# A branch for the first layer's head: order of the first products, the centring of tile 2

## The chip, the cores and the metric

The kernel runs on one core of a Trainium2 chip. The metric is the device time of one execution in microseconds, median over runs. Five engines work at once, each on its own list of instructions, and wait for each other through semaphores: TensorE (PE, with its weight loads as PEld), VectorE (DVE), ScalarE (ACT), GpSimd (POOL) and SyncE (SP), which here only issues transfers.

## The reference

A two-layer encoder on 512 tokens of 1024 channels. What bears on the change is its start: a layer norm of the input, and the input projection of the first layer.

```python
h = layer_norm(x, ln_in_g, ln_in_b)
for l in range(DEPTH):
    proj = h @ w_in[l]
    a_q, a_k, a_v, b_u, b_b, b_c, c_u, d_q, d_k, d_v = split_columns(proj)
    ...                       # four groups of heads, each RMS-normalised, side by side in mix
    h = layer_norm(DN_ALPHA * h + mix @ w_out[l], ln1_g[l], ln1_b[l])
    ffn = jnp.square(jax.nn.relu(h @ w1[l])) @ w2[l]
    h = layer_norm(DN_ALPHA * h + ffn, ln2_g[l], ln2_b[l])
```

## The kernel before

**Tiles.** The tokens lie in four tiles of 128 rows, the channels in eight blocks of 128 (kt 0 to 7). The stream x is held with tokens on the partitions; for a product it is turned by TensorE (eight transposes for a tile, four for each half of 512 channels), into PSUM banks 4 and 5, and copied from there as two operands: ScalarE casts the high part h_hi (line 860), VectorE subtracts it from the bank for the low part h_lo (line 1254). Weights come in blocks of 128 x 2048, and are split the same way: ScalarE casts w_hi (line 838, in parts of 512 columns at the start), GpSimd subtracts for w_lo (line 1708). A product of full precision is three of these: high by high, low by high, high by low weights. Block 0 of the weights serves kt 0 to 3, block 1 kt 4 to 7.

**The input norm.** Per tile VectorE takes two statistics (1201), their aggregate (1208) and the variance with its epsilon (1210); GpSimd raises it to the power -1/2 (rstd, 1687); VectorE centres and multiplies by the gain in two halves (1279) and scales and adds the bias in two halves (1284). Gain and bias stand on one partition each; TensorE spreads them to 128 rows at the start by 16 transposes (499) into banks 2 and 3 (gain) and 6 and 7 (bias). Bank 2 is where tile 2's product goes later, bank 3 tile 3's, so ScalarE copies the gain to SBUF (rows, 903), and tiles 2 and 3 centre with that copy, tiles 0 and 1 with the banks. The order by hand on VectorE: norm 0, statistics 1, low parts of tile 0, norm 1, statistics 2, low parts of tile 1, and so on; the low parts of tile 3 stand inside the layer loop, behind a wait for the parameters (cols, qk_gain) that GpSimd's queue loads.

**TensorE's order.** Behind the spreading stand 8 filler transposes (keep_warm, 493), the turn of tile 0, 6 more, and then the loop over the two layers (505). In it, tile 0 and tile 1 take their products with high weights first: for each kt the high part (521) and the low part (522), the turn of tile 1 ahead of kt 4 of tile 0. Then come the eight products with low weights of tile 0 (530), the turn of tile 2, the eight of tile 1, and tiles 2 and 3 with all three at once (449 to 451), tile 3's turn in the middle of tile 2. Both layers run this code. Tile 0 of the second layer is turned in the last chunk of the first layer's MLP, under an If on the layer (790). The MLP's middle chunks are a loop of their own (826).

**The names in the order listings.** A row is an instruction or a run of equal ones, as the compiled program has them; MATMUL stands for a weight load and its product. REGISTER_ALU and ISA are register steps that a semaphore's target takes, COMPARE_AND_BRANCH is what an If or a loop's end becomes.

## Time and profile before

| | us |
|---|---|
| median of 3 runs | 1070.64 |
| lowest and highest | 1070.27, 1070.86 |
| the profiled execution | 1070.55 |
| its span | 1068.9 |

| engine | busy, share of the span |
|---|---|
| PE | 99% |
| PEld | 84% |
| DVE | 73% |
| ACT | 49% |
| POOL | 9% |

The span runs from the first to the last instruction; 1.65 us of the profiled execution lie around it. The profile is of one execution. Its timeline gives each instruction, or run of like ones, with its start from the span's beginning and its duration; products overlap their weight loads, so for TensorE the starts of loads tell the order better than the busy time, in which a product counts 0.39 us though the next starts 0.23 later. A remark in brackets is the idle time of that engine ahead of the row and what ended it; "issue" means that nothing in the profile was waited for.

### The profile page before, as it was taken

To read this page: it belongs to the slowest core of one execution; us is meant where nothing else is said; L and a number is where in the kernel's file an instruction comes from. 1 tells how busy PE (TensorE), PEld (TensorE's weight loads), DVE (VectorE), ACT (ScalarE), POOL (GpSimd) and SP (SyncE) were. 2 spreads that over 40 slices of the span, in tenths; PEclk is the share of its full clock that TensorE was granted. 3 is DMA by queue.
4 is the path that set the end of the run, shared out by engine and by line. 5 is a ranking of instruction groups with operands and counts; after the bars stand their busy time and mean duration, and the time that the engine had idled before them with its cause. 6 is when DMAs were issued, how large, how long until landed. Compare 5 with 4: busy or idle time off the path is not lost.

```text
span 1068.9 us, 15589 instructions
## 1 busy us (share of the span) xinstructions
PE 1054.0 (99%) x5310; PEld 896.7 (84%) x5310; DVE 785.4 (73%) x1090; ACT 521.9 (49%) x784; POOL 92.6 (9%) x84
## 2 busy tenths in 40 slices
PE   8999999999999999999999999999999999999996
PEld 6888889998888888888888888899888888888885
DVE  8855886968757758758887568777794784784787
ACT  3433666365355355355634247653643643642652
POOL 5200232100000000000002003221000000000001
PEclk9999999999999999999999999999999999999998
DMA  7432013030521520431343410310234134024122
GB/s 288 158 118 78 2 61 120 2 126 32 205 79 40 179 97 31 169 115 42 117 147 134 158 40 21 118 41 23 105 120 156 40 118 158 39 98 178 40 78 80
DMA packets 17385, 105.54 MB, mean 99 GB/s; under 512 B 2019, under 2 KB 2707, under 8 KB 5795
## 3 DMA queue, kind: packets, MB, share of 16 engines
q1 hardware_dynamic: 15984, 98.70, 25.3%
q0 software_dynamic: 1184, 5.86, 1.7%
q8 instruction: 40, 0.66, 0.2%
q14 instruction: 33, 0.25, 0.1%
q10 hardware_dynamic: 144, 0.07, 0.0%
HBM read 101.49 MB, written 2.10 MB: 97 GB/s over the span
## 4 chain that ended last, share of the span: by engine, by line
PE 98%; DVE 0%; issue 0%; DVEq 0%
PE bank L449 19%; PE bank L451 18%; PE bank L450 18%; PE bank L756 10%; PE bank L758 9%; PE bank L757 9%; PE bank L699 4%; PE bank L685 2%; PE bank L458 1%; PE bank L596 1%; PE bank L597 1%; PE bank L530 1%; PE bank L609 1%; PE bank L521 1%; PE bank L522 1%; PE bank L675 0%
## 5 line engine op out<-in xcount | busy, mean ns | idle before, releaser
L449 PE MATMUL bank<-h_hi,w_hi 128*128 128x512 f32 (+1 forms) x704 | 260.6, 370 | 0.0
L450 PE MATMUL bank<-h_lo,w_hi 128*128 128x512 f32 (+1 forms) x704 | 260.3, 370 | 0.0
L451 PE MATMUL bank<-h_hi,w_lo 128*128 128x512 f32 (+1 forms) x704 | 260.3, 370 | 0.0
L756 PE MATMUL bank<-w_hi,hid_hi 128*128 128x512 f32 x448 | 174.4, 389 | 0.0
L757 PE MATMUL bank<-w_lo,hid_hi 128*128 128x512 f32 x448 | 174.3, 389 | 0.0
L758 PE MATMUL bank<-w_hi,hid_lo 128*128 128x512 f32 x448 | 174.3, 389 | 0.0
L1167 DVE TENSOR_TENSOR w_lo<-w_raw,w_hi 128x2048 fp32r<-128x2048 f32 x62 | 141.9, 2288 | 36.8 <-ACT w_hi L873 30.0
L451 PEld LDWEIGHTS bank<-h_hi,w_lo 128*128 128x128 f32 x704 | 132.6, 188 | 22.6
L450 PEld LDWEIGHTS bank<-h_lo,w_hi 128*128 128x128 f32 x704 | 132.7, 188 | 22.4
L449 PEld LDWEIGHTS bank<-h_hi,w_hi 128*128 128x128 f32 x704 | 132.6, 188 | 22.3
L873 ACT CAST w_hi<-w_raw 128x2048 fp32r<-128x2048 f32 x56 | 107.1, 1913 | 78.8 <-PE bank L758 56.4
L1581 DVE TENSOR_TENSOR x<-bank,x 128x512 f32<-128x512 f32 x112 | 74.9, 686 | 45.1 <-PE bank L758 45.1
L758 PEld LDWEIGHTS bank<-w_hi,hid_lo 128*128 128x128 f32 x448 | 84.1, 188 | 17.6
L757 PEld LDWEIGHTS bank<-w_lo,hid_hi 128*128 128x128 f32 x448 | 84.1, 188 | 17.4
L756 PEld LDWEIGHTS bank<-w_hi,hid_hi 128*128 128x128 f32 x448 | 84.1, 188 | 17.3
L1076 ACT ACTIVATE y<-bank 128x512 f32<-128x512 f32 x64 | 38.2, 597 | 105.7 <-PE bank L451 105.7
L1555 DVE TENSOR_TENSOR hid_sum<-y 128x256 f32<-128x256 f32 x64 | 24.3, 421 | 43.3 <-ACT y L1078 43.2
L1186 DVE TENSOR_TENSOR w_raw<-w_third,w_raw 128x2048 f32<-128x2048 f32 x24 | 54.8, 2285 | 1.6 <-DMA w_third<-in_weights 1.6
L1570 DVE TENSOR_TENSOR hid_lo<-hid_sum,hid_hi 128x1024 fp32r<-128x1024 f32 x32 | 39.2, 1226 | 22.4 <-ACT hid_hi L1089 22.4
L1479 DVE SCALAR_TENSOR_TENSOR x<-bank,group_r,x 128x512 f32<-128x512 f32 x64 | 46.8, 747 | 10.3 <-PE bank L451 9.5
L1684 POOL DMA_DIRECT2D rows<-in_rows x4 | 2.3, 570 | 579.7 <-DVE hid_lo L1570 579.4
L449 PE MATMUL bank<-w_hi,mix_hi 128*128 128x512 f32 x128 | 50.9, 398 | 0.0
(174 smaller groups left out, 1643.1 us busy)
## 6 DMA issues: line engine op xcount, KB each, us to landing
w_raw<-in_weights SPq DMA_DIRECT2D x63, 1024.0 KB, 4.8
w_third<-in_weights SPq DMA_DIRECT2D x23, 1024.0 KB, 4.8
rows<-in_rows POOLq DMA_DIRECT2D x4, 1024.0 KB, 5.1
w_raw<-in_weights SPq DMA_DIRECT2D x4, 512.0 KB, 7.7
out_h<-x SPq DMA_DIRECT2D x8, 256.0 KB, 2.0
x<-in_x SPq DMA_DIRECT2D x3, 512.0 KB, 9.7
dft<-in_dft SPq DMA_DIRECT2D x2, 512.0 KB, 7.1
qk_gain<-in_qk_gain POOLq DMA_DIRECT2D x3, 192.0 KB, 3.3
```

What stands on the lines that cost most here:

```text
L449: pe.matmul(dst, s_hi, m_hi, start=first, stop=False)
L450: pe.matmul(dst, s_hi, m_lo, start=False, stop=False)
L451: return pe.matmul(dst, s_lo, m_hi, start=False, stop=last)
L699: last = pe.matmul(bank[4 + (u // 4) % 2][:, c:c + HEAD_DIM], pT[:, u % 2, i * P:(i + 1) * P], v, start=(i == 0), stop=(i == k1 - k0 - 1))
L756: pe.matmul(bank[dst + t][:], s_hi, m_hi, start=start, stop=False, skip_group_check=goes_on)
L757: pe.matmul(bank[dst + t][:], s_hi, m_lo, start=False, stop=False, skip_group_check=goes_on)
L758: done = pe.matmul(bank[dst + t][:], s_lo, m_hi, start=False, stop=stop, skip_group_check=goes_on)
L873: act.copy(w_hi[:, SLOT[i], :], raw_of(i)).then_inc(sems["w_hi"], 1)
L1167: dve.tensor_tensor(w_lo[:, SLOT[i % CHUNK_OPERANDS], :], raw_of(i), w_hi[:, SLOT[i % CHUNK_OPERANDS], :].bitcast(F32), ALU.subtract).then ...
L1186: dve.tensor_tensor(dst, a, b, ALU.subtract).then_inc(sems["w_sum"], 1)
L1479: dve.scalar_tensor_tensor(out=xs, in0=b[:], scalar=group_r[:, g, t:t + 1], in1=xs, op0=ALU.mult, op1=ALU.add)\
L1581: dve.tensor_tensor(xs, bank[dst + t][:], xs, ALU.add).then_inc(sems["added"], 1)
```

## The change

It touches TensorE's order and VectorE's, and adds no computation.

- Of the 8 filler transposes ahead of tile 0's turn one is left; the 6 behind it go.
- The first products of a layer stand in two branches on the layer. The second, for l > 0, keeps the order of before, but asks for h_hi ahead of a high part and for h_lo ahead of a low part, where before h_lo was asked for ahead of both. The first, for l < 1, has an order of its own: high, low and low-weight products for kt 0 and 1, high and low for kt 2 to 7, and only then tile 1's turn; two low-weight products, all high then all low parts of tile 1, low-weight products, tile 2's turn ahead of the last six.
- VectorE takes the first low half of tile 0 between the two statistics of tile 1, and the second behind tile 1's variance.
- Tile 2 centres with the gain in banks 2 and 3, like tiles 0 and 1; tile 3 alone uses the copy.

```diff
--- before.py
+++ after.py
@@ -499,36 +499,67 @@
                         last = pe.transpose(first_row(which, half)[:, c * P:(c + 1) * P],
                                             first[:, k:k + 1].to_broadcast([P, P]), ident)
                     last.then_inc(first_spread, 1)
-            keep_warm(8)
+            keep_warm(1)
             turn(0, 0)
-            keep_warm(6)
             with pe.Fori(0, DEPTH) as l:
 
                 def first_group(t, kt):
                     c = slice(t * P, (t + 1) * P)
                     return (bank[t][:], h_hi[:, kt, c], h_lo[:, kt, c], *w_cols(kt // 4, kt % 4, BANK, 0, BANK))
 
-
-                for t in range(2):
-                    for kt in range(KT):
-                        if t == 0 and kt == 4:
-                            turn(l, 1)
+                def own_high(t, kts):
+                    for kt in kts:
+                        if kt % 4 == 0:
+                            wait(pe, l, "h_hi", 2 * t + kt // 4 + 1)
+                        if t == 0:
+                            high_part_ready(l, kt // PARTS, kt % PARTS)
+                        dst, t_hi, _, m_hi, _ = first_group(t, kt)
+                        pe.matmul(dst, t_hi, m_hi, start=kt == 0, stop=False)
+
+                def own_low(t, kts):
+                    for kt in kts:
                         if kt % 4 == 0:
                             wait(pe, l, "h_lo", 2 * t + kt // 4 + 1)
-                        if t == 0:
-                            high_part_ready(l, kt // PARTS, kt % PARTS)
-                        dst, t_hi, t_lo, m_hi, _ = first_group(t, kt)
-                        pe.matmul(dst, t_hi, m_hi, start=kt == 0, stop=False)
+                        dst, _, t_lo, m_hi, _ = first_group(t, kt)
                         pe.matmul(dst, t_lo, m_hi, start=False, stop=False)
-                for t in range(2):
-                    for kt in range(KT):
+
+                def weights_low(t, kts):
+                    for kt in kts:
                         if t == 0:
                             part_ready(l, kt // PARTS, kt % PARTS)
-                        if t == 1 and kt == 0:
-                            turn(l, 2)
                         dst, t_hi, _, _, m_lo = first_group(t, kt)
-                        last = pe.matmul(dst, t_hi, m_lo, start=False, stop=kt == KT - 1)
-                    last.then_inc(sems["products"], 1)
+                        done = pe.matmul(dst, t_hi, m_lo, start=False, stop=kt == KT - 1)
+                        if kt == KT - 1:
+                            done.then_inc(sems["products"], 1)
+
+                with pe.If(l < 1):
+
+                    own_high(0, range(2))
+                    own_low(0, range(2))
+                    weights_low(0, range(2))
+                    for kt in range(2, KT):
+                        own_high(0, (kt,))
+                        own_low(0, (kt,))
+                    turn(l, 1)
+                    weights_low(0, range(2, 4))
+                    own_high(1, range(KT))
+                    own_low(1, range(KT))
+                    weights_low(0, range(4, 6))
+                    weights_low(1, range(4))
+                    turn(l, 2)
+                    weights_low(0, range(6, KT))
+                    weights_low(1, range(4, KT))
+                with pe.If(l > 0):
+
+                    for t in range(2):
+                        for kt in range(KT):
+                            if t == 0 and kt == 4:
+                                turn(l, 1)
+                            own_high(t, (kt,))
+                            own_low(t, (kt,))
+                    weights_low(0, range(KT))
+                    turn(l, 2)
+                    weights_low(1, range(KT))
                 for t in range(2, TOK):
                     for kt in range(KT):
                         if kt == KT // 2 and t + 1 < TOK:
@@ -1267,7 +1298,7 @@
             def first_norm(t):
 
                 def row(which, half):
-                    if which or t < 2:
+                    if which or t < TOK - 1:
                         dve.wait_ge(first_spread, 2 * which + half + 1)
                         return first_row(which, half)[:]
                     dve.wait_ge(first_kept, half + 1)
@@ -1289,8 +1320,12 @@
                 row_stats(0, n)
             variance(0, 2, 1, LN_EPS)
             first_norm(0)
-            input_stats(1)
-            stream_low(0, 0, 0)
+            dve.wait_ge(x_landed[1], 16)
+            row_stats(1, 0)
+            low_half(0, 0, 0, 0)
+            row_stats(1, 1)
+            variance(1, 4, 2, LN_EPS)
+            low_half(0, 0, 0, 1)
             first_norm(1)
             input_stats(2)
             stream_low(0, 0, 1)
```

TensorE, from the end of the spreading to its first products of layer 0, before:

```order
L493 MATMUL bank<-ident_first 128x128 x8
L458 MATMUL bank<-ident_first,x 128x128 [waits normed]
L458 MATMUL bank<-ident_first,x 128x128 x3
L458 MATMUL bank<-ident_first,x 128x128 [waits normed]
L458 MATMUL bank<-ident_first,x 128x128 x3
L493 MATMUL bank<-ident_first 128x128 x6
L505 UNCONDITIONAL_BRANCH
L505 ISA
L323 ISA [waits h_lo]
L521 MATMUL bank<-w_hi,h_hi 128x512 [waits w_hi_part]
L522 MATMUL bank<-w_hi,h_lo 128x512
```

And now:

```order
L493 MATMUL bank<-ident_first 128x128
L458 MATMUL bank<-ident_first,x 128x128 [waits normed]
L458 MATMUL bank<-ident_first,x 128x128 x3
L458 MATMUL bank<-ident_first,x 128x128 [waits normed]
L458 MATMUL bank<-ident_first,x 128x128 x3
L504 UNCONDITIONAL_BRANCH
L535 COMPARE_AND_BRANCH
L323 ISA
L323 ISA [waits h_hi]
L517 MATMUL bank<-w_hi,h_hi 128x512 [waits w_hi_part]
L323 REGISTER_ALU
L517 MATMUL bank<-w_hi,h_hi 128x512 [waits w_hi_part]
```

The fillers are gone but one, a compare stands ahead of the products, and the first one waits for h_hi and a part of w_hi, with h_lo asked for behind two high parts.

VectorE from tile 0's last scaling to tile 1's centring, before:

```order
L1284 SCALAR_TENSOR_TENSOR x<-x,rstd,bank 128x512 [waits first_spread,centred]
L1201 BN_STATS bn<-x 128x6 [waits x_landed1]
L1201 BN_STATS bn<-x 128x6
L1208 BN_AGGR moments<-bn 128x2 [waits stats,x_landed1]
L1210 TENSOR_SCALAR var_eps<-moments 128x1 [waits moments]
L1254 TENSOR_TENSOR h_lo<-bank,h_hi 128x4x128 [waits h_hi] x2
L1279 SCALAR_TENSOR_TENSOR x<-x,moments,bank 128x512 [waits first_spread,moments]
```

And now:

```order
L1315 SCALAR_TENSOR_TENSOR x<-x,rstd,bank 128x512 [waits first_spread,centred]
L1232 BN_STATS bn<-x 128x6 [waits x_landed1]
L1285 TENSOR_TENSOR h_lo<-bank,h_hi 128x4x128 [waits h_hi]
L1232 BN_STATS bn<-x 128x6
L1239 BN_AGGR moments<-bn 128x2 [waits stats,x_landed1]
L1241 TENSOR_SCALAR var_eps<-moments 128x1 [waits moments]
L1285 TENSOR_TENSOR h_lo<-bank,h_hi 128x4x128 [waits h_hi]
L1310 SCALAR_TENSOR_TENSOR x<-x,moments,bank 128x512 [waits first_spread,moments]
```

The first low half has moved between the statistics, so the variance, for which GpSimd's rstd waits, has one more operation ahead of it.

TensorE at the end of layer 0's branch and the start of the other, now (before there was no such place):

```order
L531 MATMUL bank<-w_lo,h_hi 128x512 [waits w_lo_part]
L531 MATMUL bank<-w_lo,h_hi 128x512 [waits w_lo]
L531 MATMUL bank<-w_lo,h_hi 128x512 x4
L535 UNCONDITIONAL_BRANCH
L552 COMPARE_AND_BRANCH
L323 ISA
L323 ISA [waits h_hi]
L517 MATMUL bank<-w_hi,h_hi 128x512 [waits w_hi_part]
L524 MATMUL bank<-w_hi,h_lo 128x512 [waits h_lo]
```

In layer 1 the compare of line 535 jumps here, over the 128 loads and products of the first branch and some 15 register steps and waits; in layer 0 the compare of line 552 jumps over the second branch, which is as long.

## Rows read from the trace of the kernel before

**Rows 1.** Waits of TensorE, whole span: us in total, times, longest.

```profile
PE bank L521 <- DVE h_lo L1254: 0.4, 1, 0.4
PE bank L458 <- DVE x L1284: 0.4, 1, 0.4
```

**Rows 2.** Timeline, weight loads (PEld): start, us, line, operation, count, idle before.

```profile
7.64 1.72 PEld L493 LDWEIGHTS bank<-ident_first 128*128 128x128 f32 x8
9.35 1.28 PEld L458 LDWEIGHTS bank<-ident_first,x 128*128 128x128 f32 x8
...
11.91 0.19 PEld L521 LDWEIGHTS bank<-w_hi,h_hi 128*128 128x128 f32 x1 [0.63 <-issue]
...
14.40 0.42 PEld L458 LDWEIGHTS bank<-ident_first,x 128*128 128x128 f32 x4 [0.80 <-DVE x L1284]
15.06 0.42 PEld L458 LDWEIGHTS bank<-ident_first,x 128*128 128x128 f32 x4 [0.24 <-DVE x L1284]
...
17.36 0.19 PEld L521 LDWEIGHTS bank<-w_hi,h_hi 128*128 128x128 f32 x1 [0.23 <-DVE h_lo L1254]
...
22.70 1.02 PEld L458 LDWEIGHTS bank<-ident_first,x 128*128 128x128 f32 x8
...
25.40 0.19 PEld L449 LDWEIGHTS bank<-w_hi,h_hi 128*128 128x128 f32 x1
```

**Rows 3.** Timeline, VectorE (DVE), first 32 us.

```profile
7.34 1.57 DVE L1284 SCALAR_TENSOR_TENSOR x<-x,rstd,bank 128x512 f32<-128x512 f32 x2
8.83 1.28 DVE L1201 BATCH_NORM_STATS2 bn<-x 128x6 f32<-128x512 f32 x2
...
12.29 1.40 DVE L1279 SCALAR_TENSOR_TENSOR x<-x,moments,bank 128x512 f32<-128x512 f32 x2
13.61 1.40 DVE L1284 SCALAR_TENSOR_TENSOR x<-x,rstd,bank 128x512 f32<-128x512 f32 x2
...
17.82 3.37 DVE L1279 SCALAR_TENSOR_TENSOR x<-x,moments,rows 128x512 f32<-128x512 f32 x2
...
26.70 1.40 DVE L1284 SCALAR_TENSOR_TENSOR x<-x,rstd,bank 128x512 f32<-128x512 f32 x2
```

**Rows 4.** ScalarE's timeline; weight transfers: issues of line 361, time to landing.

```profile
10.47 1.07 ACT L860 CAST h_hi<-bank 128x512 fp32r<-128x512 f32 x2 [1.85 <-PE bank L458]
11.43 3.23 ACT L838 CAST w_hi<-w_raw 128x512 fp32r<-128x512 f32 x6
...
L361 SPq DMA_DIRECT2D w_raw<-in_weights x4: 424/436/440, 1.8 to 3.7; - x4
...
DMA to landing us min/median/max: 4.8/5.7/8.9
```

**Rows 5.** GpSimd's timeline (POOL); then the landing of qk_gain, last parameter.

```profile
12.14 5.04 POOL L1708 TENSOR_TENSOR w_lo<-w_raw,w_hi 128x512 fp32r<-128x512 f32 x4 [0.90 <-ACT w_hi L838]
...
17.64 3.00 POOL L1708 TENSOR_TENSOR w_lo<-w_raw,w_hi 128x512 fp32r<-128x512 f32 x2
...
21.30 0.54 POOL L1679 DMA_DIRECT2D qk_gain<-in_qk_gain  x1
...
DMA to landing us min/median/max: 6.5/6.5/6.5
```

**Rows 6.** Line 1279 by source of its gain row: ns min/median/max.

```profile
L1279 DVE SCALAR_TENSOR_TENSOR x<-x,moments,bank x4: 737/741/749, 6.0 to 12.9; 128x512 f32<-128x512 f32 x4
L1279 DVE SCALAR_TENSOR_TENSOR x<-x,moments,rows x4: 743/1208/1780, 17.8 to 26.0; 128x512 f32<-128x512 f32 x4
```

**Rows 7.** TensorE's branches, layer loop (505), chunk loop (826): ns min/median/max.

```profile
L505 PEldq COMPARE_BRANCH  x2: 76/1772/3467, 532.5 to 1055.0; - x2
...
L826 PEldq COMPARE_BRANCH  x4: 79/159/247, 368.1 to 973.4; - x4
```

**Rows 8.** Timeline, start of layer 1: weight loads, then ScalarE (ACT).

```profile
536.26 0.19 PEld L521 LDWEIGHTS bank<-w_hi,h_hi 128*128 128x128 f32 x1 [0.37 <-issue]
...
540.99 0.19 PEld L521 LDWEIGHTS bank<-w_hi,h_hi 128*128 128x128 f32 x1 [0.33 <-DVE h_lo L1254]
...
539.62 1.07 ACT L860 CAST h_hi<-bank 128x512 fp32r<-128x512 f32 x2 [1.72 <-PE bank L458]
```


## The prediction

> **What bounds the kernel now.** I began with the waits of TensorE. The reader is to see that they are almost nothing: behind the landing of its first operand only two stand in the whole span, 0.4 us each [rows 1]. TensorE's stream is therefore the bound, and a change can pay only by what it does to gaps in that stream or to its length. The order of the stream in time was read next, from the weight loads, one per product [rows 2]. It has its gaps in the head of the first layer: the first product starts at 11.91, eight products later the engine stands until 14.40 and 15.06 for the two halves of tile 1, and again until 17.36. From there on it never stands for another engine in that layer. The mark for everything below is 25.40, the first product of tile 2: what is gained there is gained to the end, unless something later becomes late. VectorE's rows show who sets those stops [rows 3]: one unbroken chain of normalisations from 8.83 to 28.10.
>
> **Durations used.** A warm product of 512 columns takes its place every 0.227 us: eight from 22.70 back to 20.88. A turn of eight transposes among them takes 0.88 more (22.70 to 25.40 is 2.70: eight products and a turn). A restart after a stop costs 0.10 once, and in a steady run a load starts one place ahead of its product. From the end of VectorE's work to TensorE's load it is 0.05 (15.01 to 15.06). The eight fillers from 7.64 to 9.35 come every 0.214 us, twice the 0.11 of later transposes, so that is the lower level, 1.2 GHz, though the granted clock is given as 1.00 throughout; the eight transposes from 9.35 take 1.28, half at either pace, so the rise falls at about 10.1. ScalarE starts its cast of a half 1.12 after the half's turn starts, where the fourth transpose was the last slow one (9.35 to 10.47); I take 1.15 for slow ones.
>
> **Part 1, tile 0's turn.** Seven of the eight filler transposes ahead of it go, and all six behind. Tile 0's halves are normalised at 8.09 and 8.91 (7.34 and 1.57 for the pair, 0.75 for the first) [rows 3], so their turns start at 8.14 and 8.96, in place of 9.35 and some 0.8 later. ScalarE casts the first half from 9.29 to 9.88 and the second from 10.11, where it cast both from 10.47 [rows 4]. Its six weight casts, 0.52 apart, start at 10.59 in place of 11.43 and end at 13.81; the fifth needs a transfer issued at 3.7 that was at most 8.9 on its way, so there by 12.6 [rows 4], and would start at 12.67. TensorE can multiply own high parts from 10.0 (only h_hi asked for), not 11.91.
>
> **Part 2, VectorE around tile 1.** The low half moves between the two statistics. VectorE does the same sum of work: first statistics from 8.83, low half at 9.91 behind ScalarE's cast (0.4 idle, much as before), second statistics to 11.20, variance at 11.53, second low half at 11.61, centring at 12.20, in place of 12.29 [rows 3]. The variance is now 1.1 later, and that is the added wait: GpSimd's rstd of tile 1 stands ahead of its low weight parts. It starts at 11.84 and delays the four parts that began at 12.14 [rows 5] by 0.22, to 12.36. They are asked for late enough: block 0 is complete at 14.9 and needed at 15.37. The rstd is there at 12.4, VectorE asks at 13.52. Tile 1 is normalised at 14.26 and 14.92, 0.09 sooner than before.
>
> **Part 3, what fits ahead of tile 1.** Before, 8 products stood ahead of its turn; now 18 do (16 own, 2 with low weights). Followed one by one: two high at 10.0, low at 10.66 once VectorE's half is out (10.60), low weights at 11.23 and 11.46, the rest from 11.69, each waiting for nothing until kt 7, whose cast ends at 13.81. The last goes in at 14.20, its slot ends at 14.43; tile 1's first half was ready at 14.31, the second's turn waits until 14.98 anyway. All ten extra products vanish into the old stop: 10 x 0.227 = 2.27. Behind that turn stand 30 products and tile 2's turn, where 40 and a turn stood. The first load is at 15.37, so the mark falls at 15.37 + 0.10 + 29 x 0.227 + 0.88 = 22.93, in place of 25.40: 2.47 sooner. Beside the ten products that is VectorE's 0.09 and some 0.1 of the stop at 17.36, which goes: high parts come first there, and the low half is out 0.4 before it is asked for. I take 2.45.
>
> **Part 4, tile 2's centring.** This is what keeps part 3 alive. With the gain row in SBUF the two operations took 3.37, from PSUM they take 1.41: singly 0.74 against up to 1.78 [rows 3, 6]. The pair from PSUM that counts is that at 12.29, which ran in the midst of GpSimd's subtractions [rows 5] and took 1.40 all the same, so I take that and no slowing. VectorE then has tile 2 normalised at 19.8 and 20.45, in place of 22.51. TensorE asks at 20.93. With the old centring it would have stood until 22.4, and 1.5 of the gain would be gone. VectorE's low half of tile 2 comes at 22.88, TensorE needs it at 22.93: no slack, but no loss. Tile 3 is normalised at 25.45 and 26.11, in place of 28.10, and asked for at 25.66 and 26.22. Next is its low half, which waits for the parameters: they land at 27.8 (issued at 21.3, 6.5 on their way) [rows 5], so it is out at 28.4, and TensorE gets there at 29.5. That is 1.0 of cover.
>
> **Part 5, the branches.** Layer 1 keeps its order but must jump over layer 0's. At its start TensorE has run dry: the jump back takes 3.47, and the first load waits until 536.26 with 0.37 idle [rows 7, 8]. So the added jumps are bare: one taken, 0.25, and one not taken, 0.08, by the chunk loop's [rows 7], with a register step or two 0.39 in all. Most of that is met by the stop at 540.99, where TensorE waits 0.33 for tile 1's low half. That half hangs on ScalarE, which starts its cast only at 539.62 after its own jump [rows 8], well behind tile 1's turn (538.7 even when late), so it stays where it is. Net 0.2 lost; bounds 0 and 0.4. In layer 0 both jumps pass while TensorE has work queued: nothing. The Trainium skill, Advanced Engine Details and Errata, Control Flow Timing, has about 0.11 for a compare-and-branch; two of them would make the net 0.05 in place of 0.2, and the rows' larger price is what I take.
>
> **Sum.** 2.45 less 0.2 is 2.25. The profiled execution took 1070.55 for a span of 1068.9; the median of the three runs is 1070.64, 0.09 above it. 1070.64 - 2.25 = **1068.4**. Bounds: the first cast 0.1 later or sooner moves the chain by as much; a clock that rises 1 us later slows up to five products and costs up to 0.4; the jump 0 to 0.4. So 1067.9 to 1069.1 for this case.
>
> **The rivals.**
> - *The clock stays low.* The fillers held TensorE busy without a break until the rise at about 10.1. Now it stands some 0.1 to 0.3 three times from 8.06 on. The Trainium skill, TensorE: Matmul & The Clock Gate, Part 1, wants sustained activity before the higher level and says that the point varies from run to run. Which of the two the trace bears out it doesn't say, since TensorE never stood there before; the stops are short. No row tells how long the low level would last. Through nine of the 18 products, at 0.45 in place of 0.227, it costs 2.0, of which waits ahead of 11.7 hide 0.5: 1069.9, the price I take. Through all 18 it is 4.1 less 0.6: 1071.9.
> - *Layer 1's branch isn't at hand.* The loop's jump back cost 3.47 because its code had to be fetched [rows 7]; the chunk loop's, whose code was there, 0.25. If the jump over layer 0's order (128 loads and multiplies and some 15 waits) leaves the code just fetched, it costs 3.47 in place of 0.25 with nothing queued: 1068.4 + 3.2 = 1071.6, slower than before. It decides from the point at which the else branch lies beyond the fetched piece; two such fetches give 1075. Against: some 145 instructions are little beside the chunk loop's 360 products with their loads, which its jump spans for 0.25. The Trainium skill, Advanced Engine Details and Errata, ISA Cache, gives 256 instructions to a line of code; by it loop start and branch would share one, and the next line would have to be there some 40 instructions on, which is narrow.
> - *The first part doesn't fit.* ScalarE's casts or the transfer behind them slip by some tenths; each tenth passes through. 0.4 to 0.8 lost: 1069.0.
> - *The centring gains nothing.* If reading PSUM beside GpSimd cost as much as SBUF, 1.5 of the gain goes: 1069.9. The pair at 12.29 speaks against it.
>
> **How the numbers follow.** Forecast 0.62, clock 0.10, branch not at hand 0.10, first part slipping 0.15, centring 0.03. A measurement tells 0.2% from no change, 2.14 us, so faster means below 1068.5, and the forecast lies just there. Of its 0.62 some 0.46 fall below that, and 0.02 of the slipping case: faster 0.48. Slower needs above 1072.8: half of the branch case, 0.05 at most. Same 0.47. The range reaches from 1067.9 to 1070.1, which leaves out the branch case and some tails.
>
> **What would show it.** In the changed profile: first product's load near 10.0; turn of tile 1 at 14.3 and 15.0 with 18 products ahead; both centrings of tile 2 at 0.74 and GpSimd's last pair of subtractions back from 3.00 to 2.55 [rows 5]; first product of tile 2 at 22.9 to 23.0 and no idle after it in that layer; in layer 1 TensorE's idle at the loop's start grown from 0.37 to 0.7 to 0.8 and the wait for h_lo gone. Wrong it is if the pace of transposes is still 0.213 beyond 10.2, if tile 2's or 3's turn shows idle for VectorE, or if more than 1 us opens around 533 to 541.

## The result: slower by 0.3%

| | before | changed |
|---|---|---|
| median, us | 1070.3 (11 runs) | 1073.87 (11 runs) |
| lowest and highest | 1069.89, 1070.86 | 1071.17, 1076.16 |
| the profiled execution | 1070.55 | 1074.24 |
| its span | 1068.9 | 1072.6 |
| mean granted clock of TensorE in it | 0.997 | 0.993 |

The ratio is 1.0029, interval 1.0021 to 1.0037. The forecast was 1068.4 and its range ended at 1070.1; the time went the other way. The runs also lie wider apart than those of before: 5.0 us instead of 1.0.

**The waits of TensorE** in the changed kernel, whole span (us in total, times, longest). Behind the landing of the first operand, where [rows 1] have two waits of 0.4, there is one big one (3.9 counts from the end of the last product; from the last load it is 4.34):

```profile
PE bank L517 <- issue: 3.9, 1, 3.9
```

"Issue" means that nothing in the profile was waited for. Where it lies, the timeline tells. First the head of layer 0: weight loads of the changed kernel (start, us, line, count, idle before), for [rows 2]:

```profile
10.06 0.40 PEld L517 LDWEIGHTS bank<-w_hi,h_hi 128*128 128x128 f32 x2 [0.30 <-issue]
10.71 0.30 PEld L524 LDWEIGHTS bank<-w_hi,h_lo 128*128 128x128 f32 x2 [0.25 <-DVE h_lo L1285]
...
13.96 0.19 PEld L517 LDWEIGHTS bank<-w_hi,h_hi 128*128 128x128 f32 x1 [0.19 <-ACT w_hi L869]
...
14.38 1.08 PEld L458 LDWEIGHTS bank<-ident_first,x 128*128 128x128 f32 x8
15.43 0.30 PEld L531 LDWEIGHTS bank<-w_lo,h_hi 128*128 128x128 f32 x2
...
23.04 0.19 PEld L449 LDWEIGHTS bank<-w_hi,h_hi 128*128 128x128 f32 x1
```

The mark, the first product of tile 2, stands at 23.04 and not at 25.40: the head has gained 2.36. A mark of one execution also holds the moment at which TensorE's clock rose in it. Two versions of experiments 2 and 3 that run the old order in the head (both_branches and skip1) had their first transposes faster and the mark at 25.07 and 24.82. So marks compare to some 0.5, unless the transposes ran alike; in the two profiles here both ran late to full pace. VectorE and GpSimd there, for [rows 3, 5]:

```profile
9.96 0.69 DVE L1285 TENSOR_TENSOR h_lo<-bank,h_hi 128x512 fp32r<-128x512 f32 x1 [0.40 <-ACT h_hi L891]
...
17.80 1.40 DVE L1310 SCALAR_TENSOR_TENSOR x<-x,moments,bank 128x512 f32<-128x512 f32 x2
...
22.27 1.29 DVE L1285 TENSOR_TENSOR h_lo<-bank,h_hi 128x512 fp32r<-128x512 f32 x2
```

```profile
11.84 0.55 POOL L1722 TENSOR_TENSOR rstd<-var_eps,half_neg 128x1 f32<-128x1 f32 x1 [1.49 <-DVE var_eps L1241]
12.37 5.06 POOL L1743 TENSOR_TENSOR w_lo<-w_raw,w_hi 128x512 fp32r<-128x512 f32 x4
...
17.90 2.54 POOL L1743 TENSOR_TENSOR w_lo<-w_raw,w_hi 128x512 fp32r<-128x512 f32 x2
```

So the head did what was forecast of it. Now the start of layer 1, for [rows 8]. Weight loads of the changed kernel:

```profile
533.38 0.19 PEld L789 LDWEIGHTS bank<-w_hi,hid_lo 128*128 128x128 f32 x1
537.90 0.29 PEld L517 LDWEIGHTS bank<-w_hi,h_hi 128*128 128x128 f32 x1 [4.34 <-issue]
538.07 0.34 PEld L524 LDWEIGHTS bank<-w_hi,h_lo 128*128 128x128 f32 x1
538.50 0.33 PEld L517 LDWEIGHTS bank<-w_hi,h_hi 128*128 128x128 f32 x1
...
542.89 0.19 PEld L517 LDWEIGHTS bank<-w_hi,h_hi 128*128 128x128 f32 x1
...
544.60 0.19 PEld L517 LDWEIGHTS bank<-w_hi,h_hi 128*128 128x128 f32 x1
```

and the two loads of the kernel before that answer to 533.38 and 542.89:

```profile
535.71 0.19 PEld L758 LDWEIGHTS bank<-w_hi,hid_lo 128*128 128x128 f32 x1
...
538.98 0.19 PEld L521 LDWEIGHTS bank<-w_hi,h_hi 128*128 128x128 f32 x1
```

What stands still is the sequencer. The branches of TensorE, as they answer to [rows 7] (ns min/median/max, then first and last start): line 504 is the loop's jump back, 535 the branch for l < 1, 552 that for l > 0.

```profile
L504 PEldq COMPARE_BRANCH  x2: 76/1944/3812, 530.2 to 1058.7; - x2
...
L535 PEldq COMPARE_BRANCH  x2: 82/1720/3357, 9.2 to 534.2; - x2
...
L552 PEldq COMPARE_BRANCH  x2: 73/154/236, 20.6 to 537.6; - x2
```

The jump back takes 3.8, much as before (3.47). Behind it the new jump over layer 0's branch takes 3357 ns, from 534.2 on, and the first load of layer 1 follows 0.4 behind its end. The last row says that the same kind of jump, over the other branch, took 236 ns in layer 0, at 20.6. On the queue that carries code (the rows don't say for which engine), one piece is moved in the stretch 535.0 to 535.5, inside those 3357 ns (packets, MB, share):

```profile
q8 instruction: 1, 0.02, 11.8%
```

In the version of experiment 1 one piece is moved between 533.5 and 534.0, again within 1.5 of the end of the jump back, but products run meanwhile. Both profiles count 40 pieces in the whole span. By these rows the changed kernel fetches no more than that version; it stands still for a piece that the other gets while it works.

Last, the clock. The same stretches of the changed kernel and of the version of experiment 1, in which TensorE doesn't stop there (us; busy and count of PE, PEld, DVE, ACT, POOL; granted clock, DMA share, GB/s):

```profile
530.00:534.00 4.00, 3.99 (x21) 3.04 (x19) 4.00 (x8) 2.16 (x4) 0.00 (x0) 1.00 0.01 4
534.00:538.00 4.00, 0.09 (x1) 0.10 (x1) 3.27 (x7) 1.52 (x4) 0.99 (x1) 0.75 0.33 78
538.00:543.00 5.00, 5.00 (x17) 4.15 (x17) 0.00 (x0) 0.42 (x1) 0.00 (x0) 0.52 0.95 372
543.00:548.00 5.00, 5.00 (x25) 4.13 (x23) 4.80 (x8) 0.76 (x2) 0.00 (x0) 1.00 0.02 8
```

```profile
534.00:538.00 4.00, 4.00 (x24) 3.37 (x23) 3.31 (x7) 2.14 (x4) 0.99 (x1) 1.00 0.37 111
538.00:543.00 5.00, 5.00 (x24) 4.12 (x23) 5.00 (x9) 0.00 (x0) 0.00 (x0) 1.00 1.03 362
```

The clock falls to the lower of its two levels (1.2 GHz, 0.50), while TensorE stands: in stretches of 0.5 us it is 1.00 up to 535.5, 0.97 in the next and 0.50 from 536.0 on, and it is back between 542.75 and 543.0. The loads behind the stop come 0.42 to 0.43 apart, where a warm product takes 0.227.

**The account**, from the loads of both profiles:

| point | before | changed | difference |
|---|---|---|---|
| first product of tile 2, layer 0 | 25.40 | 23.04 | -2.36 |
| last load of layer 0 | 535.71 | 533.38 | -2.33 |
| first load of layer 1 | 536.26 | 537.90 | +1.64 |
| first load behind eight products and a turn | 538.98 | 542.89 | +3.91 |
| first product of tile 1, layer 1 | 540.99 | 544.60 | +3.61 |
| span | 1068.9 | 1072.6 | +3.7 |

The jump costs 3.97 (1.64 and 2.33), the low clock 2.27 (4.99 instead of 2.72 for the same eight products and turn), and the stop of before at 540.99 gives 0.30 back. All 2.36 of the head arrive at the end of layer 0, and are outweighed there within five microseconds.

### The profile page after: what moved, and what is told of

Read it like the earlier page. It is cut to its first block, busy times and chain, and to the rows that moved or that the text cites. A ratio compares the mean times of both kernels' runs of the same rounds, so it can differ in the third digit from the quotient of the medians.

```text
span 1072.6 us, 15573 instructions
## 1 busy us (share of the span) xinstructions
PE 1054.5 (98%) x5297; PEld 896.7 (84%) x5297; DVE 783.6 (73%) x1090; ACT 523.3 (49%) x784; POOL 92.2 (9%) x84
## 4 chain that ended last, share of the span: by engine, by line
PE 98%; issue 1%; DMA 0%; DVE 0%; DVEq 0%
PE bank L449 18%; PE bank L450 18%; PE bank L451 18%; PE bank L788 9%; PE bank L789 9%; PE bank L787 9%; PE bank L730 4%; PE bank L716 2%; PE bank L458 1%; PE bank L627 1%; PE bank L628 1%; PE bank L517 1%; PE bank L524 1%; PE bank L531 1%; PE bank L640 1%
```

## The experiments

The theory after the two traces: the jump's target lies in a piece of code that isn't at hand in layer 1, and the fetch is bare. The rivals: the cost is that of any branch behind the jump back; the cost hangs on the length of the jump; and, for the head, that the gain isn't the order's.

### 1. The branches exchanged (swap)

The code for l > 0 now stands first, that for l < 1 behind it. The order in each layer is that of the changed kernel.

```diff
+                with pe.If(l > 0):
+                    ...       # the old order
                 with pe.If(l < 1):
                     ...       # the new order
-                with pe.If(l > 0):
-                    ...       # the old order
```

> The changed kernel with its two branches in the other sequence in the code: the one for layer 1 first, the one for layer 0 behind it. Code theory (the 3.36 us of the jump at layer 1's start and the low clock behind it are the whole loss; layer 0's part works as forecast, mark at 23.0 in place of 25.4): no jump is taken at layer 1's start, the one over layer 0's branch comes with products queued, so no idle beyond some 0.5 at the loop's start, no fall of the clock, and 1070.3 - 2.4 + 0.1 to 0.3 = 1068.1 us, with runs within 1 us of each other. Order theory (the separate waits for h_hi and h_lo in layer 1's branch, or two compares whatever their place, are the loss): it stays at 1073 to 1074 us.

1068.44 (1067.62 to 1069.54, 11 runs) beside 1070.22 of the kernel before: the ratio is 0.9983, interval 0.9974 to 0.9992. That is 1.8 faster than before and 5.4 faster than the changed kernel, by the place of two blocks of code alone. The first branch's compare and the loads at the mark and at the start of layer 1:

```profile
L535 PEldq COMPARE_BRANCH  x2: 75/216/357, 9.0 to 533.2; - x2
```

```profile
22.57 0.19 PEld L449 LDWEIGHTS bank<-w_hi,h_hi 128*128 128x128 f32 x1
...
533.53 0.19 PEld L517 LDWEIGHTS bank<-w_hi,h_hi 128*128 128x128 f32 x1 [0.46 <-issue]
...
546.29 0.19 PEld L449 LDWEIGHTS bank<-w_hi,h_hi 128*128 128x128 f32 x1 [0.20 <-DVE h_lo L1285]
```

In layer 1 nothing is jumped at the start (75 ns), and the idle is 0.46 where before had 0.37. The jump that layer 0 now makes takes 357 ns at 9.0, while VectorE and ScalarE are what TensorE waits for. The jump over the other branch at 543.2 took 336 ns with work queued. The compare that isn't taken costs 0.10 here: from the last load of layer 0 to the first of layer 1 it is 0.65, and 0.55 before. What a taken one costs with its target at hand is read in experiments 3 and 4. The jump that layer 0 makes here spans the same instructions that layer 1 jumped over in the changed kernel, and takes 357 instead of 3357 ns; it comes behind code that ran straight on and not behind a jump back. The mark of 22.57 is from the fastest of the 11 runs. From the mark to the end of the span this profile and that of before take the same to 0.2.

### 2. Two branches, nothing else (both_branches)

The kernel before, its old order written twice, once under l < 1 and once under l > 0. VectorE is untouched.

```diff
-                for t in range(2):
-                    ...       # the old order
+                with pe.If(l < 1):
+                    ...       # the old order
+                with pe.If(l > 0):
+                    ...       # the old order again
```

> The kernel before with nothing changed but that its first products stand twice, in a branch for layer 0 and one for layer 1, both in the old order. Code theory: layer 0 as before, at layer 1's start a taken compare of about 3.4 us with nothing queued, TensorE idle 3.7 to 4.4 in place of 0.37, and 0 to 2.5 more where the clock falls: 1073.5 to 1076.5 us. Order theory: 1070.3 to 1070.8 us, since the order is the old one.

1075.23 (1075.14 to 1075.26, 4 runs): ratio 1.0045, interval 1.003 to 1.0061. Its compare, its long wait, and the clock behind it:

```profile
L512 PEldq COMPARE_BRANCH  x2: 82/1500/2917, 9.2 to 536.2; - x2
```

```profile
539.52 0.19 PEld L543 LDWEIGHTS bank<-w_hi,h_hi 128*128 128x128 f32 x1 [3.93 <-issue]
...
541.11 0.33 PEld L544 LDWEIGHTS bank<-w_hi,h_lo 128*128 128x128 f32 x1
```

```profile
536.00:540.00 4.00, 0.49 (x3) 0.43 (x3) 3.28 (x7) 1.52 (x4) 0.99 (x1) 1.00 0.22 68
540.00:544.00 4.00, 4.00 (x17) 3.43 (x16) 0.33 (x1) 0.69 (x2) 0.00 (x0) 0.61 1.03 364
```

The branches alone cost 5.0, with no change of order at all. So the loss belongs to them; experiment 1, which keeps the new waits in layer 1 and loses nothing at its start, says the same. Here the clock falls some 1.4 after the restart and not during the stop: the first products still run at the full pace.

### 3. How far the jump goes (skip1, skip30, skip90)

The kernel before, with fillers under an If at the head of the loop, which layer 1 jumps over: 1, 30 or 90 transposes, which are 2, 60 or 180 instructions.

```diff
             with pe.Fori(0, DEPTH) as l:
+                with pe.If(l < 1):
+                    keep_warm(1)      # 30, 90
```

> The kernel before with one filler transpose under an If for layer 0 at the head of the layer loop, so that layer 1 takes a jump over two instructions right behind the jump back. Theory of the piece of code (a jump costs 3.4 only where its target lies outside the piece just fetched): the compare takes about 0.25, TensorE's idle there grows from 0.37 to about 0.6, 1070.4 to 1070.7 us. Rival (any taken jump that close behind the jump back has to wait for the fetch of the next piece, which is then on its way): the compare takes about 3.4 here too, 1073.5 us or more.

> The kernel before with 30 filler transposes, 60 instructions, under an If for layer 0 at the loop's head. Layer 0 runs them: up to 3.3 us more less what lies in the wait for tile 0 there. What tells is the compare in layer 1. Piece-of-code theory: the target, some 60 instructions on, lies in the piece just fetched, so 0.25 (with 2 instructions it was 0.246, with 180 it was 3.23). Theory that the cost grows with distance: about 1.2.

> The same with 90 filler transposes, 180 instructions, under the If. Layer 0 runs them, 90 x 0.109 = 9.8 us more, so the time is 1080 us and more in any case; what tells is the compare in layer 1. Both theories of the jump: about 3.4 us, and TensorE idle about 4. If it takes 0.25 the loss in the changed kernel is no matter of distance.

The times are 1070.27, 1072.38 and 1083.36, single runs, in which layer 0's fillers count too. What tells is the compare, one row for each kernel in this order, and the first load behind it:

```profile
L512 PEldq COMPARE_BRANCH  x2: 85/166/246, 9.2 to 535.8; - x2
```

```profile
L512 PEldq COMPARE_BRANCH  x2: 85/166/246, 9.3 to 537.9; - x2
```

```profile
L512 PEldq COMPARE_BRANCH  x2: 85/1658/3232, 9.3 to 544.2; - x2
```

```profile
536.25 0.19 PEld L523 LDWEIGHTS bank<-w_hi,h_hi 128*128 128x128 f32 x1 [0.93 <-issue]
```

```profile
547.73 0.19 PEld L523 LDWEIGHTS bank<-w_hi,h_hi 128*128 128x128 f32 x1 [4.06 <-issue]
```

A jump over 2 and one over 60 instructions cost the same 246 ns, one over 180 costs 3232. It is a step and no slope, so neither a branch as such nor its nearness to the jump back costs 3 us. The short one isn't free: the idle grew from 0.37 to 0.93, where about 0.6 had been expected, and from the last load of layer 0 to the first of layer 1 it is 1.12 instead of 0.55. The stop at 540.99 is gone in that profile and gives 0.30 back, so 0.3 is lost. The time of this run, 1070.27, doesn't show the loss, since its mark in layer 0 came at 24.82 by a sooner rise of the clock. The longest of the three doesn't say whether the length decides or the place; experiment 4 does.

### 4. The same jump, all code shifted (after_pad)

The changed kernel, with 88 fillers ahead of the layer loop. The branches and the length of the jump, some 143 instructions, are those of the changed kernel.

```diff
             turn(0, 0)
+            keep_warm(88)
             with pe.Fori(0, DEPTH) as l:
```

> The changed kernel with 88 filler transposes (176 instructions of load and multiply) ahead of the layer loop, nothing else. The branches keep their order, the jump in layer 1 its length of 143 instructions. The fillers take some 10 (88 x 0.114) in the head, so the time itself says nothing; layer 1's start does. Theory (what counts is whether the jump's target lies in the same piece of code as the loop's start): so far a target up to 145 instructions from the program's start was at hand and one 198 or more from it wasn't, so a piece ends in between; if pieces are 256 long, as the time between fetches in the long stretches suggests, the next one ends at 401 to 454. With the fillers the loop starts at 230 and the target lies at 374, both in that piece: the compare of the first branch takes about 0.25 in layer 1, the idle ahead of the first product 1.1 to 1.3, and the granted clock stays up behind it. Rival (what counts is the length of the jump, 143 or more against 60 or less): it takes 2.9 to 3.4 as in the changed kernel, the idle is over 4, and the clock falls.

The branch's compare in layer 1, the first load behind it, and the clock:

```profile
L536 PEldq COMPARE_BRANCH  x2: 85/167/249, 17.4 to 542.4; - x2
```

```profile
543.07 0.19 PEld L518 LDWEIGHTS bank<-w_hi,h_hi 128*128 128x128 f32 x1 [0.90 <-issue]
```

```profile
544.00:548.00 4.00, 4.00 (x24) 3.37 (x23) 3.53 (x7) 1.24 (x4) 0.99 (x1) 1.00 0.64 196
```

It takes 249 ns instead of 3357 for the same jump, the idle is 0.90 (1.1 to 1.3 had been expected) instead of 4.34, and the clock stays at 1.00. With the length unchanged, the place decides; each of these compares was seen in one execution. The 1077.08 of this kernel (one run, 1069.84 for before beside it) holds 9.64 us of fillers, so it is no version to keep. The expectation had put the end of a piece between the 145th instruction from the program's start (the target of skip30, at hand) and the 198th (that of the changed kernel, not at hand); these counts are good to a few instructions. The length of 256 was an assumption, and the outcome fits it: a next end at 401 or later leaves both the loop's start at 230 and the target at 374 in one piece. It would fit any length above some 176 as well. The Trainium skill, Advanced Engine Details and Errata, ISA Cache, gives a line of code as 16 KB and 256 instructions; the trace agrees with the size, since 40 packets on the code queue are 0.66 MB, 0.0165 each; the number of instructions is only bounded by the runs, as said.

### 5. Which part of the head carries the gain

All of these start from the version of experiment 1 or from the kernel before, or have no branch, so that no fetch covers what they show. Four of them undo one part each, one adds two fillers, and one does VectorE's part alone.

**The fillers back (swap_fillers).**

```diff
-            keep_warm(1)
+            keep_warm(8)
             turn(0, 0)
+            keep_warm(6)
```

> The exchanged branches (swap, 1068.44 us with runs from 1067.6 to 1069.5) with the filler transposes back: 8 ahead of tile 0's turn, 6 behind. Chain theory: the turn starts at 9.35 in place of 8.2, so ScalarE's cast, VectorE's low half and with it the whole chain to tile 1's normalisation come 1.1 later, and the mark (first product of tile 2) at 24.1 in place of 23.0: 1069.5 us. Clock theory of the spread (without fillers the clock rises in some runs later, and that is the 2 us between the runs of swap): the runs lie within 0.8 us of each other, and the median is no more than 0.5 above swap's.

1068.8 (1068.12 to 1069.38, 11 runs), ratio 0.9986, interval 0.9977 to 0.9995: 0.4 more than without them, within the spread of both. Its first product and its mark:

```profile
10.25 0.30 PEld L518 LDWEIGHTS bank<-w_hi,h_hi 128*128 128x128 f32 x2
...
23.19 0.19 PEld L449 LDWEIGHTS bank<-w_hi,h_hi 128*128 128x128 f32 x1
```

The 1.1 that the expectation had given for the fillers didn't show in the time, and the mark is 0.6 later. The rival, that the fillers narrow the runs to within 0.8 of each other, didn't come true either: they lie 1.3 apart. In this execution the transposes came at the higher level sooner: the eight fillers took 1.09 where [rows 2] have 1.72, and the turn followed at 8.73. How much the fillers cost should hang on when the clock rises, which is argued and not shown; by the pace of the transposes that moment differs between the profiles of this case by more than 2 us (from before 7.5 to about 10.1).

**Two fillers behind tile 0's turn (swap_two).**

```diff
             turn(0, 0)
+            keep_warm(2)
```

> The version with the two branches exchanged, with 2 filler transposes behind tile 0's turn. The rise of the granted clock comes anywhere from 7.3 to 10.1 in the executions profiled so far. If the stops around tile 0's turn sometimes hold the rise back, two fillers close one of them, and the spread of the runs (1.9 with none, 1.3 with 14 fillers) falls without a later mark: median 1068.2 to 1068.5. If the spread comes from elsewhere, it stays at 1.3 to 1.9 and the median moves by less than 0.4, since the fillers fit ahead of ScalarE's cast (first product at 10.06 to 10.25).

1068.58 (1067.94 to 1070.58, 11 runs), ratio 0.9986, interval 0.9977 to 0.9995, mark 22.77. The spread is 2.6, no smaller than without them. That the stops around tile 0's turn hold the clock back now and then isn't borne out.

**Tile 2 centred with the copy in SBUF, as before (swap_rows).**

```diff
-                    if which or t < TOK - 1:
+                    if which or t < 2:
```

> The exchanged branches with tile 2 centred from the copy in SBUF, as before the change. Port theory: the pair of centrings takes 3.3 to 3.4 in place of 1.40, tile 2 is normalised at 22.4, TensorE stands for it 1.4 to 1.6 at its turn: 1068.4 + 1.5 = 1069.9 us. Rival (TensorE would find cover in the order of the rest): within 0.3 of 1068.4 us.

1070.24 (1069.53 to 1071.1, 10 runs), ratio 1.0, interval 0.9991 to 1.0009: the whole gain is gone, 1.8 of it. VectorE, then TensorE:

```profile
17.70 3.17 DVE L1310 SCALAR_TENSOR_TENSOR x<-x,moments,rows 128x512 f32<-128x512 f32 x2
```

```profile
21.59 0.42 PEld L458 LDWEIGHTS bank<-ident_first,x 128*128 128x128 f32 x4 [1.31 <-DVE x L1315]
...
24.54 0.19 PEld L449 LDWEIGHTS bank<-w_hi,h_hi 128*128 128x128 f32 x1 [0.68 <-DVE h_lo L1285]
```

The two operations take 3.17 beside GpSimd's subtractions and 1.40 from the bank at the same place. The forecast had put this at 1.5; it is a little more, since the late low half stops TensorE a second time. GpSimd's pair of subtractions beside it takes 2.98 in this run, and 2.54 in the changed kernel. The Trainium skill, SBUF — State Buffer, Who interferes with whom, says that GpSimd and an operation of VectorE with two SBUF inputs shut each other out while GpSimd's reads SBUF; with the gain row in PSUM only one input is left there. The traces agree, with 3.17 against 1.40 and 2.98 against 2.54.

**VectorE's order of before around tile 1 (swap_dve).**

```diff
-            dve.wait_ge(x_landed[1], 16)
-            row_stats(1, 0)
-            low_half(0, 0, 0, 0)
-            row_stats(1, 1)
-            variance(1, 4, 2, LN_EPS)
-            low_half(0, 0, 0, 1)
+            input_stats(1)
+            stream_low(0, 0, 0)
```

> The version with the two branches exchanged, with VectorE's order of before around tile 1 (both statistics and the variance ahead of tile 0's low halves). Chain theory: TensorE asks for the first low half right behind two high parts (first low product at 10.71 in the changed kernel) and it is out only at about 11.2, as before, so TensorE stands some 0.5 there and everything behind slips by as much: tile 1's turn from 14.4 to 14.9, the first product of tile 2 from 23.0 to 23.5, and the median 0.5 above the exchanged version. Rival, slack theory: ScalarE's weight casts (to 13.8) and VectorE's second half of tile 1 hold the stream anyway, the 0.5 vanishes into them and mark and median stay.

1069.48 (1068.48 to 1071.43, 10 runs), ratio 0.9993, interval 0.9984 to 1.0002:

```profile
11.10 0.30 PEld L524 LDWEIGHTS bank<-w_hi,h_lo 128*128 128x128 f32 x2 [1.04 <-DVE h_lo L1285]
...
23.29 0.19 PEld L449 LDWEIGHTS bank<-w_hi,h_hi 128*128 128x128 f32 x1
```

TensorE stands 1.04 for the low half of tile 0, and the mark is 0.7 later than in experiment 1 (22.57); the median is 1.0 higher, though the two spreads overlap. The expectation had 0.5 for both the stop and the median. The stop is longer because the first product came at 9.74 and not at 10.06.

**VectorE's part alone (dve_only).** The kernel before, with its TensorE order, and VectorE's two changes.

> The kernel before, with only VectorE's two changes: its order around tile 1, and tile 2 centred from the banks. TensorE keeps its old order. Theory (the two sides only pay together): tile 1 is normalised 0.09 sooner and the low half of tile 1 in time, so the mark 25.40 moves to 25.2 to 25.3 and the median by 0.1 to 0.2 at most. Rival (VectorE's part carries a share of the 2.4 alone): mark 0.5 or more below 25.40.

1070.67 (1070.09 to 1071.75, 10 runs), ratio 1.0005, interval 0.9996 to 1.0014, mark:

```profile
25.13 0.19 PEld L449 LDWEIGHTS bank<-w_hi,h_hi 128*128 128x128 f32 x1
```

The mark is 0.27 sooner than in the profile of before, which is within what the moment of the clock's rise does to it (skip1 has 24.82 with VectorE's old work), and there is nothing in the time. So VectorE's part alone shows no gain. Of TensorE's order each of VectorE's two changes, undone singly in the two experiments above, takes 1.8 and about 1.0, the second with overlapping spreads. TensorE's order with both of them undone wasn't run.

**Layer 0's order in both layers, no branch (one_order).**

```diff
-                with pe.If(l < 1):
-                    ...
+                ...           # the new order, in both layers
-                with pe.If(l > 0):
-                    ...       # the old order
```

> The changed kernel without branches: layer 0's order runs in both layers. Layer 1 has its low weight parts from VectorE at 536.4 to 543.9 and tile 1's turn would come 2.9 later there. Theory that layer 1 has room for it: no jump, no fetch, 1068.3 to 1069.0 us. Theory that layer 1 needs its own order (the reason a branch would be wanted): VectorE's chain in layer 1 slips by the 2.4 and more by which the turn and the cast behind it are later, TensorE stands for tile 2 or 3 there, 1070.5 us or more.

1069.92 (1069.24 to 1071.2, 10 runs), ratio 0.9998, interval 0.9989 to 1.0007. The mark is at 22.71, so the head has its gain, and in layer 1:

```profile
548.22 0.19 PEld L449 LDWEIGHTS bank<-w_hi,h_hi 128*128 128x128 f32 x1 [1.69 <-DVE h_lo L1273]
```

The new order asks for the low half of tile 2 before VectorE has it in layer 1, which costs 1.7; the median is 1.5 above that of experiment 1. So the two layers want orders of their own, and the exchange of experiment 1 makes the branch affordable.

## Why the prediction was wrong

**Parts 1 to 4, the head: right.** First product forecast at 10.0, measured 10.06; turn of tile 1 14.31, measured 14.38; the first load behind it 15.37, measured 15.43; rstd of tile 1 11.84 and low weight parts 12.36, measured 11.84 and 12.37; tile 2's centring 1.41, measured 1.40; GpSimd's last pair 2.55, measured 2.54; mark 22.93, measured 23.04. The low half of tile 2 had no slack and caused no stop. Experiments 1 and 5 show the centring at work, and with less certainty VectorE's order; that the fillers' removal pays isn't shown. Of the 0.11 that is missing at the mark, 0.06 is there at the first load behind tile 1's turn, and 0.05 comes in the 7.6 us behind it.

**Part 5, the branches: this step failed.** The term was 0.39 bare, 0.2 net, since it had the jump's target at hand. It measured 3.97 bare, and 5.94 net, with 2.27 for the clock and 0.30 given back. The rival "Layer 1's branch isn't at hand" described the mechanism and its place, and its price of 3.47 for the fetch was near the 3.36 of the row; it was given 0.10. Two inferences held it down.

- *The comparison with the chunk loop.* Its jump spans 360 products for 0.25 [rows 7], and 145 instructions looked little beside that. But that jump goes back to code which has just run, and the code queue moved nothing in the loop's second pass (368 to 450), whereas this one goes forward, behind a jump back that itself had to fetch. The code ahead of the target hadn't run in this layer, so nothing had brought it in. That this is the reason is argued from the pieces on the code queue. Experiment 4 shows that the length alone doesn't decide: the same 143 instructions cost 249 or 3357 ns.
- *The place of the boundary.* Whether two points lie in one piece depends on where the program's instructions fall, and the change takes 26 of them away ahead of the loop (13 fillers of two) and adds some 150 in it. I took it that the loop's start and the jump's target share a piece, and never counted from the program's start in the changed order. A piece ends between the 145th and the 198th instruction; the target is at 198 in the changed kernel. In the exchanged one the layer that has to start bare begins at 54, where the jump back lands.

**The clock: a term that wasn't there.** I had priced a low clock in the head, where it didn't stay, and none behind the rival's stop. The fall costs 2.27. With it the rival's own sum is 1071.6 + 2.3 = 1073.9, and the median is 1073.87; so close a match is partly luck, since the account of the profiled execution ends at 1074.2, and the clock doesn't seem to fall in every run. Without the fall the account gives 1070.64 - 2.33 + 3.97 - 0.30 = 1072.0, and the two runs with the highest mean clock (0.998) are at 1071.17 and 1071.78, while four of the five from 1073.88 up to 1076.16 show 0.993 in the mean and one 0.995. That fits a fall which comes in most executions and not in all. It wasn't taken apart further, since only one execution of the changed kernel has a timeline. The longest run, 1076.16, has a span of 1072.8, hardly more than the profiled one: 3.4 us of it lie outside the span, where before had 1.65. What they are stays open.

**The stop at 540.99.** It was to take up most of the branches' price. It gives back 0.30 in both cases: of the 0.57 of a short jump (skip1), and of 3.97. So for a target at hand the forecast's 0.39 bare was low (0.57, 0.73 in skip30, and 0.54 with both compares in experiment 4), and its net of 0.2 about right.

## The better version

The exchanged branches run in 1068.44, 0.17% under the kernel before and 0.5% under the changed one. The forecast for branches at hand had been 2.25 less than before; measured are 1.8, with an interval from 0.9 to 2.8. Where the 0.4 between them goes, if it is real, isn't shown: the profile of this version is of its fastest run.

## What to carry to other kernels

A branch is cheap only if its target is at hand, and even then it took 0.5 to 0.7 here where the engine had nothing queued. Directly behind a loop's jump back, put the code that this trip runs first and without a jump, and let the trip that has slack, here layer 0 with its engines still waiting for the first norm, do the jumping. Where a branch has to stay, read the duration of the compare on its engine, which shows a fetch as 3 us in place of 0.25, and count the instructions from the program's start, knowing that here the pieces' ends were only bracketed; a stop of that length should be priced together with the clock that it may cost behind it.

## What was not expected of the hardware

- A taken branch at the layer's start costs 222 to 357 ns with its target at hand (336 and 357 in experiment 1, 222 to 249 in the others), whether it spans 2, 60 or 143 instructions, and 2917 to 3357 ns with a fetch. Not taken it is 73 to 85. With nothing queued, the next load comes 0.54 to 0.73 later for a taken one with its target at hand (after_pad, skip1, skip30). The Trainium skill, Advanced Engine Details and Errata, Control Flow Timing, has about 108 ns for a compare-and-branch; the rows lie on both sides of it, lower for one not taken and two to over three times as high for one taken.
- TensorE's granted clock fell to its lower level at a stop of 3.9 to 4.3 us: from 536.0 to about 542.8 in the changed kernel, the last 4.9 of them at unbroken work, and from about 540.9 to 544.3 in experiment 2. It rose by itself, with TensorE at work. With stops of 0.5 to 1.1 at the same place it stayed at 1.00.
- The fall can begin after work has resumed: in experiment 2 the first products behind the stop came at the full pace, and the loads turned slow some 1.4 us later.
